# Input in column quarters, the first weight slab alone, and TensorE turning two slabs ahead in the first group

## What is computed

```python
h = rms_norm(x, norm_g[l]).astype(x.dtype)
z = jnp.einsum('bsd,dn->bsn', h, w_in[l])
(q_r, k_r, v_r, gate_r, ...) = jnp.split(z, split_idx, axis=-1)
```

## Time and profile before

| | |
|---|---|
| median of 3 runs | 983.94 us (982.16 to 984.73) |
| profiled execution | 983.71 us |
| span of its instructions | 981.9 us |
| granted TensorE clock, mean | 0.997 |
| PE busy | 949.2 us (97%) |
| ACT busy / DVE busy / POOL busy | 405.4 / 419.4 / 472.8 us |

### The profile page before, as it was taken

How to read it: one execution, slowest core, us unless ns; L and a number is a source line. 1 busy time by engine, 2 the same in 40 slices (tenths; PEclk the granted TensorE clock), 3 DMA queues, 4 the chain that set the end, 5 groups by cost and what they waited for, 6 DMA issues and landing times.

```text
span 981.9 us, 13086 instructions
## 1 busy us (share of the span) xinstructions
PE 949.2 (97%) x4792; PEld 769.8 (78%) x4792; DVE 419.4 (43%) x998; ACT 405.4 (41%) x892; POOL 472.8 (48%) x448
## 2 busy tenths in 40 slices
PE   5999999999999999999999999999999989999998
PEld 5878788887888878777777877789888866777777
DVE  3300138144114433765655433325657664465531
ACT  5332342334224343455455422236544454555531
POOL 3443445534546744664344343344557738534342
PEclk9999999999999999999999999999999989999999
DMA  6433221322333332222212142323334311100013
GB/s 204 121 88 86 67 63 44 94 79 86 107 98 95 86 86 81 71 65 65 57 52 65 66 172 66 105 85 90 101 83 122 107 61 47 44 14 9 23 43 107
DMA packets 41168, 78.71 MB, mean 80 GB/s; under 512 B 3297, under 2 KB 5089, under 8 KB 41105
## 3 DMA queue, kind: packets, MB, share of 16 engines
q1 hardware_dynamic: 40240, 76.30, 25.9%
q10 hardware_dynamic: 864, 1.57, 0.5%
HBM read 75.74 MB, written 2.12 MB: 79 GB/s over the span
## 4 chain that ended last, share of the span: by engine, by line
PE 86%; DVE 6%; ACT 3%; POOL 3%; issue 2%; DMA 1%; SPq 1%; ACTq 0%; DVEq 0%; POOLq 0%
PE Z L1583 23%; PE Z L1585 22%; PE Z L1584 22%; PE A L1808 4%; PE A L1816 2%; PE A L1710 2%; PE A L1723 2%; PE A L1593 1%; PE A L1583 1%; PE A L1776 1%; PE A L1585 1%; PE A L1584 1%; DMA raw<-in_w_in 1%; POOL w_lo L815 1%; PE A L1736 1%
## 5 line engine op out<-in xcount | busy, mean ns | idle before, releaser
L815 POOL TENSOR_TENSOR w_lo<-raw,w_hi 128x512 fp32r<-128x512 f32 (+1 forms) x262 | 341.8, 1313 | 414.9 <-ACT w_hi L522 414.6
L1583 PE MATMUL Z<-w_hi,hT_hi 128*128 128x512 f32 (+1 forms) x832 | 338.1, 406 | 4.7 <-DVE tmp L1126 1.6
L1585 PE MATMUL Z<-w_hi,hT_lo 128*128 128x512 f32 (+1 forms) x832 | 324.0, 389 | 0.0
L1584 PE MATMUL Z<-w_lo,hT_hi 128*128 128x512 f32 (+1 forms) x832 | 323.5, 389 | 0.0
L522 ACT CAST w_hi<-raw 128x512 fp32r<-128x512 f32 (+1 forms) x262 | 157.5, 615 | 266.1 <-PE Z L1585 244.3
L1583 PEld LDWEIGHTS Z<-w_hi,hT_hi 128*128 128x128 f32 x832 | 156.4, 188 | 47.1 <-issue 9.0
L1585 PEld LDWEIGHTS Z<-w_hi,hT_lo 128*128 128x128 f32 x832 | 156.2, 188 | 32.6
L1584 PEld LDWEIGHTS Z<-w_lo,hT_hi 128*128 128x128 f32 x832 | 156.8, 188 | 26.6
L1583 PE MATMUL Z<-w_hi,oT_hi 128*128 128x512 f32 x128 | 51.3, 401 | 1.6 <-DVE tmp L1126 1.1
L639 ACT ACTIVATE x_sb<-x_sb,nmax 128x128 f32<-128x128 f32 (+3 forms) x64 | 35.5, 557 | 38.3 <-DVE nmax L1270 38.3
L1585 PE MATMUL Z<-w_hi,oT_lo 128*128 128x512 f32 x128 | 50.0, 391 | 0.0
(11 more groups left out here) (220 smaller groups left out, 1379.2 us busy)
## 6 DMA issues: line engine op xcount, KB each, us to landing
raw<-in_w_in SPq DMA_DIRECT2D x92, 512.0 KB, 3.8
raw<-in_w_out SPq DMA_DIRECT2D x16, 512.0 KB, 3.7
raw<-in_ret_w_o SPq DMA_DIRECT2D x8, 512.0 KB, 3.3
raw<-in_diff_w_o SPq DMA_DIRECT2D x8, 512.0 KB, 3.4
x_sb<-in_x SPq DMA_DIRECT2D x8, 256.0 KB, 6.1
x_sb<-in_x SPq DMA_DIRECT2D x4, 512.0 KB, 4.6
out<-x_sb SPq DMA_DIRECT2D x8, 256.0 KB, 3.3
raw<-in_w_in SPq DMA_DIRECT2D x4, 416.0 KB, 3.3
```

The costliest lines, as they stand in the source:

```text
L815: pool.tensor_tensor(w_lo[:, s % SPLIT_SLOTS, 0:width], raw[:, c % RAW_SLOTS, s - CHUNK_START[c], 0:width], w_hi[:, s % SPLIT_SLOTS, 0:wid ...
L1583: pe.matmul(out, l_hi, r_hi, start=first, stop=False)
L1584: pe.matmul(out, l_hi, r_lo, start=False, stop=False)
L1585: return pe.matmul(out, l_lo, r_hi, start=False, stop=last)
```

## The change

SP first issues x in four transfers of 512 rows by 256 columns (quarters), with a semaphore each. Between them stand the constants and chunk 0, which is loaded in two transfers of one slab each; slab 0 has a semaphore of its own. The order is: quarter 0, ident, slab 0, cols_in, quarter 1, slab 1, small, chunk 1, quarters 2 and 3, and the other constants.

TensorE does turns 0 and 1 ahead of slab 0 and turn k+2 behind slab k, for k from 0 to 5. Each even turn waits for its quarter. ScalarE follows: after turned 0, hi 0, turned 1, hi 1 and hi 2 it does for each k from 2 to 7 turned k, hi k+1, and from k = 4 on one row square. VectorE does row_rms after block 7 instead of after block 3. The second layer's `row_squares` is written differently, with the same instructions.

```diff
-        x_loaded = [sem("x_loaded0"), sem("x_loaded1")]
+        x_loaded = [sem(f"x_loaded{i}") for i in range(4)]
...
+            def x_quarter(i):
+                cc = slice(256 * i, 256 * (i + 1))
+                sp.dma_start(x_sb[:, :, cc], a["x"][0, :, cc].rearrange("(t p) c -> p t c", p=P)).then_inc(x_loaded[i], 16)
+
+            x_quarter(0)
             sp.dma_start(ident[:, :], a["c_ident"]).then_inc(c_loaded, 16)
+            sp.dma_start(raw[:, 0, 0, :], a["w_in"][0:P, 0:512]).then_inc(raw_first, 16)
             sp.dma_start(cols_in[:, :], a["cols"]).then_inc(c_loaded, 16)
+            x_quarter(1)
+            sp.dma_start(raw[:, 0, 1, :], a["w_in"][P:2 * P, 0:512]).then_inc(raw_ready[0], 16)
             sp.dma_start(small[:, :], a["c_small"]).then_inc(c_loaded, 16)
-            for half in range(2):
-                for t in range(TT):
-                    sp.dma_start(x_sb[:, t, 512 * half:512 * half + 512],
-                                 a["x"][0, P * t:P * (t + 1), 512 * half:512 * half + 512]).then_inc(x_loaded[half], 16)
-                if half == 0:
-                    chunk(0)
-
             chunk(1)
+            x_quarter(2)
+            x_quarter(3)
...
+                if g == 0:
+                    hi(2)
+                    for k in range(2, KD):
+                        turned(hT_hi[:, k, :], turn_gain(g, k))
+                        if k + 1 < KD:
+                            hi(k + 1)
+                        if k >= 4:
+                            if k == 4:
+                                for i in range(4):
+                                    act.wait_ge(x_loaded[i], 16)
+                            row_square(0, k - 4)
+                    continue
...
-                        if k == 3 and g in (0, G_LAYER2):
+                        if k == (KD - 1 if g == 0 else 3) and g in (0, G_LAYER2):
                             row_rms(int(g > 0))
...
+                if g == 0 and k % 2 == 0:
+                    pe.wait_ge(x_loaded[k // 2], 16)
...
-                for k in range(4 if g in TURNED and g not in EARLY else 0):
+                for k in range(0 if g not in TURNED or g in EARLY else 2 if g == 0 else 4):
                     turn_when_ready(g, k)
...
-                    elif g in TURNED and g not in EARLY and k < 4:
+                    elif g == 0 and k < KD - 2:
+                        turn_when_ready(g, k + 2)
+                    elif g == G_LAYER2 and k < 4:
                         turn_when_ready(g, k + 4)
```

More of the change, by code:

```diff
@@ L303, in build @@
         out_done = sem("out_done")
-        raw_ready = [sem("raw_ready0"), sem("raw_ready1")]
+        raw_first, raw_ready = sem("raw_first"), [sem("raw_ready0"), sem("raw_ready1")]
         hi_ready, lo_ready, slab_used, z_ready = sem("hi_ready"), sem("lo_ready"), sem("slab_used"), sem("z_ready")
@@ L518, in hi @@
                 width = GROUPS[g][2]
-                act.wait_ge(raw_ready[c % RAW_SLOTS], 16 * (c // RAW_SLOTS + 1))
+                if s == 0:
+                    act.wait_ge(raw_first, 16)
+                else:
+                    act.wait_ge(raw_ready[c % RAW_SLOTS], 16 * (c // RAW_SLOTS + 1))
                 if s >= SPLIT_SLOTS:
@@ L572, in turned, with row_square @@
                 count["t"] += 1
+            def row_square(layer, t):
+                c = 4 * layer + t
+                act.activation(o_sb[:, t, :], x_sb[:, t, :], ACT.Square,
+                               accum_out=acc[:, c:c + 1]).then_inc(acc_ready, 1)
             def row_squares(layer):
+                act.wait_ge(z_by_dve, dve_evacs[G_LAYER2])
+                act.wait_ge(t_lo, 32)
                 for t in range(TT):
[L577 to L582, removed]
+                    row_square(layer, t)
             def retention(stage):
@@ L772, in _ @@
                     dst = turn_dst[TURNED[g][1]][0]
-                    for k in range(2 if g == 0 else 4, 4) if g in (0, *EARLY) else range(4):
+                    for k in range(0 if g in EARLY else 4):
                         turned(dst[:, k, :], turn_gain(g, k))
[L775 to L781, removed]
+                    if g == G_LAYER2:
+                        row_squares(1)
                 for k in range(3, n):
@@ L1836, in turn_when_ready @@
                 half = k // 4
[L1837 to L1840, removed]
+                if g == 0 and k % 2 == 0:
+                    pe.wait_ge(x_loaded[k // 2], 16)
+                if k % 4 == 0 and g:
+                    if g == G_RET_OUT:
                         pe.wait_ge(th_used, 4 * (half + 1))
```

## The result

The changed kernel takes 987.72 us in the median of 11 executions (985.28 to 988.74), the kernel before 982.16 us in 11 beside it (981.13 to 985.14). The ratio is 1.0046, with a 95% interval from 1.0034 to 1.0057: slower by about half a per cent. The forecast was 988.0 us and 0.4%, and the range held the time.

The account below looks back on a forecast made before the run. TensorE, busy 949.2 of 981.9 us, was taken to bound the kernel. +0.3 +0.9 -0.65 +2.4 +1.35 = +4.3 us on the profiled 983.71 gave 988.0 us, 0.4% slower, range 984.2 to 990.6.

Parts of the forecast that it names:

- first matmul of slab 0: At the start: small lands at 9.85 behind 1640 KB, so the first matmul comes at 13.8, 0.3 us later.
- slab 0 slow after the hole: Slab 0: TensorE idles about 2.1 us before it, so half its matmuls run slow, +1.35 us (bounds 0 and 2.7).
- two more turns between slabs: Group 0: two turns move from the initial wait to behind the first matmul, +0.9 us (bounds 0.7 and 1.2).
- stall of block 4 gone: Before slab 4: row_rms no longer stands ahead of the fifth hT_lo on VectorE, -0.65 us (bounds 0.41 and 0.65).
- stall at group 1: Group 0's eviction waits for row_rms, now after the last turn, two instructions held by GpSimd: +2.4 us (0.3 to 3.5).
- The lower bound that the text gave: Earliest landing of small: 1.68 MB at 300 GB/s from 1.6 on, and about a microsecond to land, 8.3.
- The clock column: Start: granted clock 1.00 says no clock was withheld, giving +2.95 us; the skill page's throttling rule gives the adopted +4.3.
- the constants did not overtake: First rival: small lands about 2 us after issue, first matmul near 9.3, 4.2 us earlier; 983.5 us; chance 0.12.
- the norm was not in time: Rival: w_lo of slabs 8 and 9 miss row_rms, group 1 stalls only 0.3; +2.2, 985.9 us; chance 0.13.
- the slab was slow: Rival denied here: no slow slab 0, clock column right or eight transposes enough; +2.95, 986.7 us; chance 0.18.
- The premise that what is lost before group 1 goes through to the end: TensorE is busy 97%, so a microsecond won or lost before group 1's first matmul reaches the end.

Follow-up runs that it names:

- the constants first: The changed kernel with ident, cols_in and small issued ahead of x quarter 0; 982.93 us, ratio 1.0014 to the kernel before.
- the four edits that keep its order of transfers: The changed kernel with row squares early (1.0042), four turns ahead of slab 0 (1.0007), eight idle transposes before slab 0 (1.0040), or w_hi of slabs 8 and 9 earlier (1.0036).
- the filled hole: The changed kernel with eight idle identity transposes between turn 1 and slab 0; 986.57 us, ratio 1.0054; timed again 985.84 us, 1.0040.
- the early squares: The changed kernel with the four row squares behind w_hi of slab 2 and row_rms behind block 2; 987.73 us, 1.0052; again 985.72 us, 1.0042.
- The version with the hole at the attention filled: The changed kernel with constants first and four turns ahead, plus 28 idle transposes at the start of the second layer's attention; 980.19 us, ratio 0.9971.
- the version that it is built on: The changed kernel with the constants issued first and four turns ahead of slab 0; 980.44 us, ratio 0.9973 to the kernel before.
- TensorE kept busy from the start: The changed kernel with constants first and four turns ahead, plus ten idle transposes between the constants' landing and turn 0; 981.02 us, ratio 0.9980.

## Why the prediction came out right, step by step

Counted at the first matmul of group 1, in the two profiled executions:

| step | forecast, us | measured, us | from |
|---|---|---|---|
| first matmul of slab 0 | +0.3 | -0.69 | 12.83 against 13.52 |
| slab 0 slow after the hole | +1.35 | +1.56 | 4.91 against 3.35 |
| two more turns between slabs | +0.9 | +0.94 | growth of the difference over slabs 4 to 6 |
| stall of block 4 gone | -0.65 | -0.66 | difference before slab 4, 0.88, and at it, 0.22 |
| stall at group 1 | +2.4 | +2.28 | 36.62 to 41.62 against 2.72 |
| sum | +4.3 | +3.4 | 41.62 against 38.18 |

The table uses one more line of TensorE's timeline of the kernel before, the start of slab 7:

```profile
35.46 0.39 PE L1583 MATMUL Z<-w_hi,hT_hi 128*128 128x512 f32 x1
```

**The start.** The mechanism was right: small released TensorE, and with the constants first x did. The size had the wrong sign, by 1 us. The failed step is the landing time that was taken over from weight chunk 0: the same 1640 KB had landed at 10.9 there and were expected at 9.85 here; small landed at 8.97. The estimate took one landing in one execution for a property of the queue. Over nine traces, of the changed kernel and of the four edits that keep its order of transfers, TensorE's release lay between 8.48 and 9.29 us, so even the repeat moves by 0.8 us. What made the landing earlier than chunk 0's was not tried. The lower bound that the text gave, 8.3 (its terms add to 8.2), was nearer than its middle.

**Slab 0.** Right, and shown by the filled hole. Half the slab was a guess whose size was partly luck: eight of twelve matmuls were slow in this trace, but over the seven traces that keep the hole it is seven to all twelve, and slab 0 takes 1.4 to 2.6 us longer than before.

**Turns and the old stall.** Right to 0.05 us; each came from a row of the same operation in the same place.

**The norm.** Right in place, cause and size: the fourth square ends 2.0 us after slab 6 begins (2.15 expected), row_rms takes 4.9 us (35.80 to 40.70, 4.9 expected), two instructions are held. What gave the size was to ask what ScalarE does right behind the last square, and whom that sets going: w_hi of slabs 8 and 9, hence GpSimd.

**The clock column.** The granted clock in the row for the start read 1.00, and by it the slow slab should not have been. Here too it reads 1.00 (third column from the end) while the matmuls stand 0.43 us apart, the spacing that they have where the column reads 0.50 (last section):

```profile
13.00:16.50 3.50, 3.50 (x9) 2.73 (x10) 0.00 (x0) 0.00 (x0) 2.15 (x2) 1.00 0.99 301
```

This 1.00 is no measurement. The trace holds no entry of the clock before 16.57 us, and the column shows 1.00 where nothing was recorded; the first entry, 1.00, comes just where the slow matmuls end (16.38, 16.70). In the kernel before it comes at 13.89, behind the one slow matmul, and with the hole filled at 11.77, ahead of the first. So the prediction read the earlier trace rows wrongly when it set the column against the durations. The filled hole decides: idle work removed the slow matmuls. That agrees with the rule of the Trainium skill that the prediction set against the column (page "TensorE: Matmul & The Clock Gate", section "Part 1: The HAM clock gate").

**The rivals.** None took place: the constants did not overtake, the norm was not in time, the slab was slow. In the first rival, a start near 5 gives a first matmul near 8.8, not 9.3, by the 3.82 us from 9.70 to 13.52; with the constants first it was 3.81 us (6.08 to 9.89). This did not enter the forecast.

**From group 1 to the end.** The premise that what is lost before group 1 goes through to the end held: the difference stays at 3.6 us until the clock falls in one of the two traces. In the second trace of the early squares the clock falls at the same place as in the kernel before; group 1 begins 2.16 us later there, and the span is 2.3 us longer.

**The time.** That 988.0 lies 0.3 us beside the median is in good part luck. The forecast adds 4.3 us to 983.71, the profiled execution, which is 1.6 us above the median of eleven; the medians differ by 5.6 us, 1.3 us more than forecast. These two errors cancel. In the traces the sum at group 1 was not too low, as in the medians, but 0.9 us too high. The clock explains only part of the way from 3.4 to 5.6: among executions with a mean clock of 0.999 or more, the changed kernel's median is 985.67 us (four) and that of the kernel before, run beside the experiments, 981.27 (fifteen), 4.4 us less; at 0.997 it is 988.22 (seven) against 983.14 (eleven), 5.1 us. The rest stays open. Slab 0 differs from execution to execution, and the mean clock leaves out the start, where nothing is recorded. The one trace of the kernel before is of an execution 0.6 us slower than the median of those with its mean clock.

## What to carry to other kernels

When large transfers are moved to the front of a queue, look for the smallest transfer that any first instruction waits for: it now stands behind them, and the big ones win little: the first matmul came 0.7 us earlier here, and 3.6 us earlier with the constants first. When a short chain of tiny instructions is moved to the end of a stage, ask which engine is set going in the same moment; here two meetings with GpSimd made 2.0 of 2.1 us of stall, and the late squares by themselves some 0.2. Work that fills a wait is free only there, and it may also be what keeps TensorE fast for the work behind the wait.

## What the runs showed of the hardware that was not expected

The time of every kernel here spreads over 3 to 5 us, and part of the cause can be seen: the clock falls behind a hole in the second layer's attention in some executions and not in others. The profiled execution of before, and that of the changed kernel, have the same hole of 3.00 us there. TensorE's timeline of the kernel before, and its busy time and granted clock (third column from the end) in a stretch behind the hole:

```profile
799.78 0.55 PE L1583 MATMUL A<-kT_hi,qT_hi 128*128 128x256 f32 x1 [3.00 <-DVE q_lo L1331]
...
802.26 0.63 PE L1584 MATMUL Z<-hT_lo,w_hi 128*128 128x512 f32 x1
802.69 0.63 PE L1585 MATMUL Z<-hT_hi,w_lo 128*128 128x512 f32 x1
```

```profile
800.00:801.00 1.00, 1.00 (x6) 1.00 (x7) 0.77 (x4) 1.00 (x3) 0.00 (x0) 0.50 0.00 0
```

The same two views of the changed kernel:

```profile
803.39 0.36 PE L1599 MATMUL A<-kT_hi,qT_hi 128*128 128x256 f32 x1 [3.00 <-DVE q_lo L1347]
...
804.72 0.39 PE L1600 MATMUL Z<-hT_lo,w_hi 128*128 128x512 f32 x1
804.94 0.39 PE L1601 MATMUL Z<-hT_hi,w_lo 128*128 128x512 f32 x1
```

```profile
803.00:804.00 1.00, 0.60 (x5) 0.64 (x6) 0.97 (x5) 0.39 (x2) 0.00 (x0) 1.00 0.03 8
```

At 0.50, the level of 1.2 GHz, the products start 0.43 us apart, at 1.00, the level of 2.4 GHz, 0.22; the fall costs the kernel before 1.8 us. In these two kernels the times go with the mean clock of each execution: the kernel before, in 62 executions beside the experiments, has a median of 981.20 us in the ten executions with a mean clock of 1.000, and 984.89 us in the ten with 0.995. The changed kernel has 985.28 to 985.84 us in the four with 0.999 or more and 987.55 to 988.74 us in the seven with 0.997. The clock is not the whole cause. The version with the hole at the attention filled has mean clocks of 0.998 and 1.000 alone, and still reaches from 977.83 to 982.31 us. In its trace quarter 1 landed 5.8 us after its issue and group 1 began at 35.45; in the version that it is built on it was 5.1 and 34.07, and with TensorE kept busy from the start 6.8 and 36.15, from the same place in the queue. So the landing of the input moves the start from trace to trace. A kernel of this length can so move by a third of a per cent without any change of its code, nearly as much as the change studied here. Which executions keep the clock was not found.
